# Banded attention with a context part: from a loop over head pairs to 16 unrolled steps of one block

## The chip, the cores and the metric

The kernel runs on one core of a Trainium2 chip. The metric is the device time of one launch in microseconds (us), the median of several runs. PE is the matrix engine (TensorE), DVE the vector engine, ACT the scalar engine, SP the engine whose queue issues the DMAs, PEld the loading of weights into PE.

## What is computed

The program is one inference step of a two-layer trunk with a width of 1024, for 512 latent and 128 context tokens (640 columns in all). Every layer has a gated feed-forward part, a mixer, and a second feed-forward part. The mixer of layer 0 has one input projection of 21 tiles of 128 columns: 4 tiles of attention queries (8 heads of 64, two heads a tile), 1 of keys, 1 of values (2 key/value heads), and 15 that belong to a recurrent mixer (RWKV-7). The attention part, cut to what matters:

```python
# queries in blocks of 128; keys: all context keys, a sink logit per head, and the
# latent keys of the block before, the same and the next one, masked to +-128 tokens
s_ctx = einsum("bqkgd,blkd->bkgql", qi, k_ctx) * scale
s_win = einsum("bqkgd,blkd->bkgql", qi, kw) * scale
parts = [where(valid, s_win, -inf), s_ctx, sink_s]
p = softmax(concatenate(parts, axis=-1), axis=-1)
out = einsum(p_win, vw) + einsum(p_ctx, v_ctx)      # latent queries and keys are rotated first
```

The 128 context tokens attend to context keys only and are not rotated. The recurrent mixer shifts its own 15 tiles by one token both ways (`_token_shift`). Both outputs go through one output projection.

## The kernel before, in words

Activations lie with channels on the 128 partitions and the 640 tokens along the free dimension. Every product with a weight matrix goes slab by slab (128 output columns): SP loads the slab, ACT and DVE split it in a high and a low part (`split_hi`, `split_lo`), PE makes 48 matmuls of 320 columns, and a consumer takes the result out of the accumulator banks (`pp[0]` to `pp[3]`, two banks each). Slabs lie in rings of four.

In the input projection of layer 0 (`AB_COLUMN` gives the order of its columns: queries, then the 15 recurrent tiles, then keys and values last), ACT takes a result to a padded buffer `praw` (L2167 to L2169), and DVE forms the token shift from it for all 21 tiles (L2410, L2414; for attention tiles the shift weights are 0). `ab_shift` counts these operations.

Attention is written by hand with semaphores; each engine works its own list in order. PE (`pe_attn_ab`) first waits for the last shifted tile, turns context keys and values (L377, L378, L380), copies keys to both halves of the partitions by matmuls with tables (L383 to L389), and then loops over 4 head pairs. In one turn of the loop it makes the rotated partner of the queries by a matmul (L397), the scores of one head of the pair for all four blocks and the context (L409 to L411), those of the other head, and per head 15 turnings of 128x128 in two parts (L420) and 15 products with the values (L435). DVE (`dve_attn_ab`) rotates the queries (L505 to L508), scales and masks the scores into SBUF (L514, L516), takes the maxima (L522), and divides the exponentials by their sums (L530 to L536). ACT takes exponentials (L467), copies turned maps (L475, L477, L478) and writes the result (L490, L491). Each stage handles a whole head, and the scores of the next turn of the loop wait for the end of the one before.

After attention comes the recurrent mixer. SP (`sp_rwkv`) loads its masks (L651) and its starting states (L653) once attention has ended; the first work of PE there (L857) waits for both.

The mixer of layer 1 (`pe_attn_c` and its partners, L1664 to L1956) is not changed. It already works in 32 unrolled steps of one block, with the turning three steps behind the scores, and rotates by DMA from partition to partition (L1652) with DVE operations inside its input projection. It comes into the prediction as the nearest thing to measure by.

Of the kernel before, what the change touches and what calls it, by code (L numbers as in the profile page):

```python
# [54 lines left out]
AB_COLUMN = [0, 1, 2, 3] + list(range(6, 21)) + [4, 5]  # L55
# [80 lines left out]
def build(nc, T):  # L136
    ctx = ExitStack()
    with ctx:
# [197 lines left out]
        a_keys = hh[:, 0:1280].rearrange("p (g n) -> p g n", g=2)  # L336
        a_pkeys = hh[:, 1280:1536].rearrange("p (g n) -> p g n", g=2)
        a_vtok = hh[:, 1536:2176].rearrange("p (t n) -> p t n", n=P)
        a_vpast, a_kpast = hh[:, 2176:2304], hh[:, 2304:2432]
        a_kpast_t, a_kout = hh[:, 2432:2560], hh[:, 2560:2688]  # L340
        a_sink = hh[:, 2688:2696]
        a_q, a_qp = hh[:, 2700:3212], hh[:, 3212:3340]
        a_t1, a_t2 = hh[:, 3340:3852], hh[:, 3852:4364]

        a_max, a_neg, a_es, a_den, a_rden = ([hh[:, o + 8 * i:o + 5 + 8 * i] for o in (4400, 4448)] for i in range(5))
        a_sk = hh[:, 4440:4442]
        a_s, a_e = ([o[:, q:q + 2560].rearrange("p (b n) -> p b n", b=5) for o in (hl, work)] for q in (0, 2560))
        a_pt = wh[:, 0:2048]
# [3 lines left out]
        PIECES = [(b, i) for b in range(NB) for i in range(ENDS[b] // P)] + [(NB, 0)]  # L352

        a_load, a_pe, a_act, a_dve, a_out = (sem(f"a_{n}") for n in ("load", "pe", "act", "dve", "out"))
        APE0 = Steps(a_pe, ["past_t", "v_t", "dup", "dup2"])
        AAC0 = Steps(a_act, ["past_t", "v_t", "dup2"])
        ADV0 = Steps(a_dve, ["mul0", "keys0", "mul1", "keys1"])
        APE = Steps(a_pe, ["rot", "sc0", "sc1", "ta0", "tb0", "pv0", "ta1", "tb1", "pv1"], 4)
        AAC = Steps(a_act, ["qp", "exp0", "pa0", "exp1", "pb0", "o0", "pa1", "pb1", "o1"], 3)
        ADV = Steps(a_dve, ["rope1", "rope", "s0", "mx0", "ng0", "s1", "dn0", "rd0", "pn0", "mx1", "ng1", "dn1", "rd1", "pn1"], 4)  # L360
        HALF_PIECES = 8
        IN_AB = start["in", 0, 0, 0]
        IN_C = start["in", 1, 0, 0]

        def sp_attn_ab(sp):
            sp.wait_ge(slab_used, IN_AB + AB_TILES + RING)
            sp.dma_start(a_vpast, T["cache_a_v"][0, 0].rearrange("t g d -> t (g d)")).then_inc(a_load, 16)
            sp.dma_start(a_kpast, T["cache_a_k"][0, 0].rearrange("t g d -> t (g d)")).then_inc(a_load, 16)
            sp.dma_start(a_sink, T["a_sink"].to_broadcast([P, AH])).then_inc(a_load, 16)
            sp.wait_ge(a_act, AAC0.value("v_t"))  # L370
            sp.dma_start(T["new_a_k"][0, 0].rearrange("t g d -> t (g d)"), a_kout).then_inc(a_out, 16)
            sp.dma_start(T["new_a_v"][0, 0].rearrange("t g d -> t (g d)"), a_vtok[:, 4, :]).then_inc(a_out, 16)

        def pe_attn_ab(pe):
            pe.wait_ge(a_load, 48)
            pe.wait_ge(ab_shift, 3 * AB_TILES)
            nc.tensor.transpose(pp[0][:, 0, 0:P], a_kpast, ident)  # L377
            nc.tensor.transpose(pp[0][:, 0, P:2 * P], big[:, T_KA, LAT:TOK], ident).then_inc(APE0.sem("past_t"), 1)  # L378
            for t in range(NCH):
                ins = nc.tensor.transpose(pp[1][:, t // 4, (t % 4) * P:(t % 4 + 1) * P], big[:, T_VA, t * P:(t + 1) * P], ident)  # L380
            ins.then_inc(APE0.sem("v_t"), 1)
            for g in range(2):
                nc.tensor.matmul(pp[2][:, g, :], dup[g], big[:, T_KA, 0:LAT], start=True, stop=True)  # L383
                ins = nc.tensor.matmul(pp[3][:, g, :], rdup[g], big[:, T_KA, 0:LAT], start=True, stop=True)
            ins.then_inc(APE0.sem("dup"), 1)
            pe.wait_ge(a_act, AAC0.value("past_t"))
            for g in range(2):
                nc.tensor.matmul(pp[0][:, g, 0:P], dup[g], a_kpast_t, start=True, stop=True)
                ins = nc.tensor.matmul(pp[0][:, g, P:2 * P], dup[g], big[:, T_KA, LAT:TOK], start=True, stop=True)  # L389
            ins.then_inc(APE0.sem("dup2"), 1)  # L390

            for g in range(2):
                with pe.Fori(0, 2) as jj:
                    it = jj + 2 * g
                    pe.wait_ge(a_act, AAC.before(it) - 1)
                    pe.wait_ge(a_dve, ADV.before(it))
                    nc.tensor.matmul(pp[2][:, 0, :], rot, big[:, it, 0:LAT], start=True, stop=True).then_inc(APE.sem("rot"), 1)  # L397
                    for h in range(2):
                        r = slice(h * HD, h * HD + HD)
                        if h == 0:  # L400
                            pe.wait_ge(a_dve, ADV.value("rope", it))
                            pe.wait_ge(a_act, AAC.value("qp", it))
                        else:
                            pe.wait_ge(a_dve, ADV.value("s0", it))
# [2219 lines left out]
```

## Time and profile before

| what | us |
| --- | --- |
| runs | 3267.14, 3279.99, 3290.77 |
| median | 3279.99 |
| the profiled execution, its own time | 3279.32 |
| its span, first to last instruction | 3277.5 |
| its PE busy / DVE busy / ACT busy | 3026.0 / 1618.2 / 934.7 |

The profile is of one execution. Times in it count from the start of its span. Matmuls of 32-bit floats appear as two records each (so "x30" in rows of L435 is 15 matmuls, and "x2" of L410 one); turnings appear as one. "PEclk" is the clock granted to PE as a share of 2.4 GHz: 1.00 and 0.50 are the two levels, and a value between them is a stretch with both.

### The profile page before, as it was taken

How to read it: one execution, taken by the hardware profiler on the slowest of the kernel's cores; microseconds unless marked ns; L12 is line 12 of the kernel's file. 1: busy time of each engine (PE TensorE's matmuls, PEld its weight loads, DVE VectorE, ACT ScalarE, POOL GpSimd, SP SyncE). 2: the span in 40 equal slices, each digit the busy share in tenths (PEclk: the TensorE clock that was granted, in tenths of full speed). 3: DMA queues.
4: the chain of work that ended last, by engine and by line, in shares of the span. 5: the costliest groups of instructions: out<-in, count | busy, mean ns of one | idle time of the engine just before them, and what ended most of it. 6: DMA issues, size and time to landing. Idle time of an engine off the chain costs nothing.

```text
span 3277.5 us, 65384 instructions
## 1 busy us (share of the span) xinstructions
PE 3026.0 (92%) x28476; PEld 2886.5 (88%) x28476; DVE 1618.2 (49%) x2444; ACT 934.7 (29%) x1597; POOL 0.2 (0%) x4
## 2 busy tenths in 40 slices
PE   7799999997669888899999999999999888999998
PEld 7799999995557776799999999999999668999998
DVE  2455465653445565455454656454633674422324
ACT  1221212322244342231222322212322573322222
POOL 0000000000000000000000000000000000000000
PEclk6799999997668899899999999999999899999999
DMA  6344454220000000234444344443342202222221
GB/s 207 91 111 127 115 142 116 71 58 4 0 19 5 5 6 5 84 97 133 124 123 116 103 116 122 116 135 110 105 112 71 59 1 65 74 74 71 77 77 58
DMA packets 394624, 270.71 MB, mean 83 GB/s; under 512 B 12315, under 2 KB 373046, under 8 KB 394294
## 3 DMA queue, kind: packets, MB, share of 16 engines
q1 hardware_dynamic: 394422, 267.74, 29.2%
q8 instruction: 161, 2.64, 0.3%
q14 instruction: 41, 0.34, 0.0%
HBM read 257.61 MB, written 4.06 MB: 80 GB/s over the span
## 4 chain that ended last, share of the span: by engine, by line
PE 87%; DVE 7%; ACT 3%; issue 2%; DMA 1%; SPq 0%; DVEq 0%; ACTq 0%
PE banks L2509 66%; PE banks L2533 2%; PE banks L1679 2%; PE banks L2464 2%; PE banks L843 1%; PE banks L435 1%; PE banks L410 1%; PE banks L826 1%; PE banks L1731 1%; DVE big L2309 1%; PE banks L837 1%; PE banks L2540 1%; PE banks L420 1%; DVE h_lo_as_f L1423 1%; PE banks L2519 1%
## 5 line engine op out<-in xcount | busy, mean ns | idle before, releaser
L2509 PE MATMUL banks<-h_hi,w_hi 128*128 128x320 f32 x3600 | 822.1, 310 | 11.5 <-DVE w_lo L2208 10.9
L2509 PE MATMUL banks<-h_lo,w_hi 128*128 128x320 f32 x3600 | 821.2, 309 | 0.0
L2509 PE MATMUL banks<-h_hi,w_lo 128*128 128x320 f32 x3600 | 820.4, 309 | 0.0
L2509 PEld LDWEIGHTS banks<-h_hi,w_hi 128*128 128x128 f32 x3600 | 602.0, 188 | 12.7 <-issue 11.7
L2509 PEld LDWEIGHTS banks<-h_lo,w_hi 128*128 128x128 f32 x3600 | 602.8, 188 | 0.0
L2509 PEld LDWEIGHTS banks<-h_hi,w_lo 128*128 128x128 f32 x3600 | 602.8, 188 | 0.0
L2509 PE MATMUL banks<-big_as_f32r,w_hi 128*128 128x320 f32 x2816 | 530.9, 310 | 5.8 <-DVE w_lo L2208 5.3
L2208 DVE TENSOR_TENSOR w_lo<-raw,w_hi 128x1024 fp32r<-128x1024 f32 x333 | 399.0, 1218 | 193.3 <-ACT w_hi L2088 192.6
L2088 ACT ACTIVATE w_hi<-raw 128x1024 fp32r<-128x1024 f32 x333 | 341.6, 1050 | 445.5 <-DMA raw<-ffn_w 290.4
L2509 PEld LDWEIGHTS banks<-big_as_f32r,w_hi 128*128 128x128 f32 x2816 | 443.7, 189 | 6.8 <-DVE w_lo L2208 6.1
L2353 DVE TENSOR_TENSOR work<-work,banks 128x640 f32<-128x640 f32 x88 | 72.2, 821 | 607.1 <-PE banks L2509 593.1
L2509 PE MATMUL banks<-big_as_f32r,w_lo 128*128 128x320 f32 x1408 | 321.9, 310 | 0.0
L2289 DVE SCALAR_TENSOR_TENSOR big<-work,cols,big 128x1024 f32<-128x1024 f32 x240 | 296.4, 1278 | 0.0
L2142 ACT ACTIVATE big_as_f32r<-work 128x640 f32 (+1 forms) x88 | 65.0, 739 | 616.4 <-DVE work L2353 616.4
L2509 PEld LDWEIGHTS banks<-big_as_f32r,w_lo 128*128 128x128 f32 x1408 | 236.4, 189 | 0.0
L2382 DVE SCALAR_TENSOR_TENSOR x<-banks,mod,x 128x320 f32<-128x320 f32 x336 | 127.0, 433 | 212.6 <-PE banks L2509 212.1
L2140 ACT ACTIVATE work<-banks 128x640 f32<-128x640 f32 x88 | 62.0, 704 | 281.3 <-PE banks L2509 250.6
L2356 DVE TENSOR_TENSOR big_as_f32r<-work,big_as_f32r 128x640 f32 (+1 forms) x88 | 72.7, 826 | 88.9 <-ACT big_as_f32r L2142 88.9
L2155 ACT ACTIVATE work<-x 128x640 f32<-128x640 f32 x48 | 35.5, 739 | 204.4 <-DVE x L2382 204.4
L2533 PE MATMUL banks<-h_hi,w_hi 128*128 128x320 f32 x192 | 52.0, 357 | 28.6 <-DVE w_lo L2208 17.5
L1679 PE MATMUL banks<-h_hi_as_f,big 64*128 64x512 f32 (+3 forms) x256 | 68.8, 527 | 8.6 <-issue 5.2
L2533 PEld LDWEIGHTS banks<-h_hi,w_hi 128*128 128x128 f32 x192 | 38.8, 228 | 30.2 <-DVE w_lo L2208 17.7
(354 smaller groups left out, 2744.6 us busy)
## 6 DMA issues: line engine op xcount, KB each, us to landing
raw<-ffn_w SPq DMA_DIRECT2D x272, 512.0 KB, 5.2
work<-mod_w SPq DMA_DIRECT2D x136, 512.0 KB, 3.8
raw<-w_in_c SPq DMA_DIRECT2D x24, 512.0 KB, 3.9
raw<-w_in_ab SPq DMA_DIRECT2D x21, 512.0 KB, 4.0
w_hi_as_f<-mod_w SPq DMA_DIRECT2D x8, 512.0 KB, 4.9
raw<-w_out_ab SPq DMA_DIRECT2D x8, 512.0 KB, 5.2
work<-big SPq DMA_DIRECT2D x64, 64.0 KB, 2.7
raw<-w_out_c SPq DMA_DIRECT2D x8, 512.0 KB, 5.3
```

The costliest lines, as they stand in the source:

```text
L1679: return mm(c_scores(b)[:, m, a:z], big[heads[m], h, b * P:(b + 1) * P], c_keys[h][heads[m], a:z], start=True, stop=True)
L2088: nc.scalar.activation(w_hi[:, j % RING, :, :], raw[:, j % RING, :, :], ACT.Copy).then_inc(hi_full, 1)
L2140: nc.scalar.activation(silu_t, pp[(n0 + 2 * e) % 4][:, :, 0:HALF], ACT.Silu).then_inc(silu_done, 1)
L2142: nc.scalar.activation(halves2(g_hi, 2 * i + e), prod_t, ACT.Copy).then_inc(ghi_done, 1)
L2208: nc.vector.tensor_tensor(w_lo[:, j % RING, :, :], raw[:, j % RING, :, :], f32(w_hi[:, j % RING, :, :]), ALU.subtract).then_inc(lo_full, 1)
L2289: nc.vector.scalar_tensor_tensor(out=sm, in0=sec_ring[:, e, :], scalar=cols3[:, k + (C_COND + DT * g), :], in1=sm, op0=ALU.mult, op1=ALU.a ...
L2353: nc.vector.tensor_tensor(prod_t, silu_t, pp[(n0 + 2 * e + 1) % 4][:, :, 0:HALF], ALU.mult).then_inc(pair_free, 2)
L2356: nc.vector.tensor_tensor(halves2(g_lo, 2 * i + e), prod_t, f32(halves2(g_hi, 2 * i + e)), ALU.subtract).then_inc(g_ready, 1)
L2382: ins = nc.vector.scalar_tensor_tensor(out=x[:, j, a:b2], in0=src, scalar=mod[:, gate + j, g:g + 1], in1=x[:, j, a:b2], op0=ALU.mult, op1= ...
L2464: ins = nc.tensor.matmul(pp[2 + j // 4][:, 0, 2 * (j % 4):2 * (j % 4) + 2], mod_ring[:, j % RING, k, :], cond[:, k, :], start=(k == 0), st ...
L2509: ins = nc.tensor.matmul(ps[:, c, 0:HALF], w, v[:, k, c * HALF:(c + 1) * HALF], start=(k == 0 and w is hi and v is xh), stop=(k == kts - 1 ...
L2533: nc.tensor.matmul(pp[j % 4][:, c, 0:HALF], w[:, j % RING, k, :], h_hi[:, k, c * HALF:(c + 1) * HALF], start=(k == 0 and w is w_hi), stop= ...
```

## The change

- The projection makes queries, keys and values first (`A_ORDER`, slabs 0 to 5); ACT copies these six straight into `big`, without token shift. The 15 recurrent tiles follow, with the shift as before.
- Queries and keys are rotated inside the projection: SP copies the partner rows of each tile with 8 DMAs (L395), DVE makes three operations of 512 columns for one tile (L540 to L544) at each of slabs 6 to 10. Keys are copied to both halves of the partitions by four DMAs (L401). The matmuls with tables go.
- Attention is 16 unrolled steps: one block of 128 queries for both heads of a pair. PE turns the map of step g-3, makes scores of step g, then multiplies values of step g-3. DVE adds the mask in the banks, takes a negated maximum of both heads in one operation, and scales the exponentials of step g-2. ACT copies out step g-4, the turned map of g-3, and takes exponentials of g-1 straight from the banks. The context queries of a pair ride on its fourth block.
- The masks and states of the recurrent mixer are loaded as soon as the last slab of the projection has been used; PE and DVE wait for the last result of attention by `A_END`.

```diff
-AB_COLUMN = [0, 1, 2, 3] + list(range(6, 21)) + [4, 5]
+        A_ORDER = [0, 1, 2, 3, T_KA, T_VA] + list(range(4, T_KA))
+        def sp_in_ab(sp, j):
...
+            i = j - 8
+            if 0 <= i < 5:
+                sp.wait_ge(pair_free, IN_AB + i + 1 + RING)
+                if i > 1:
+                    sp.wait_ge(ADR.s, ADR.value("q", i - 2))
+                for g in range(8):
+                    o = (g ^ 1) * 16
+                    sp.dma_start(a_rt[i % 2][g * 16:g * 16 + 16, :], big[o:o + 16, A_ORDER[i], 0:LAT]).then_inc(a_rot[i % 2], 16)
...
+            def scores(g):
+                it, b = a_at(g)
+                kv = it // 2
+                if g >= 2:
+                    it2, b2 = a_at(g - 2)
+                    pe.wait_ge(AAE.s, AAE.value(f"e{b2}", it2))
...
+                for h in range(2):
+                    r = heads[h]
+                    q, ps = big[r, it, b * P:(b + 1) * P], a_scores(g)[:, h, :]
+                    if joined:
+                        ins = mm(ps[:, 0:ENDS[b]], q, a_keys[r, kv, 0:ENDS[b]], start=True, stop=True)
+                    else:
+                        ins = mm(ps[:, P:ENDS[b]], q, a_keys[r, kv, P + k0 * P:P + k1 * P], start=True, stop=True)
...
+            def turn(g):
+                it, b = a_at(g)
+                pe.wait_ge(ADN.s, ADN.value(f"p{b}", it))
...
+                for h in range(2):
+                    for c in range(4 if b else 3):
+                        ins = tp(A_TURN[:, h, c * P:c * P + P], a_e[g % 2][:, h, c * P:c * P + P], ident)
...
+            def values(g):
...
+                for i, (c, t) in enumerate(ps):
+                    v = a_vpast[:, kv] if t is None else a_vtok[:, t, kv]
+                    for h in range(2):
+                        ins = mm(a_result(g)[heads[h], 0:P], v, a_pt[g % 2][:, h, c:c + P], start=(i == 0), stop=(i + 1 == len(ps)))
...
+            for g in range(ASTEPS + ALAG):
+                if g >= ALAG:
+                    turn(g - ALAG)
+                if g < ASTEPS:
+                    scores(g)
+                if g >= ALAG:
+                    values(g - ALAG)
...
+            def exps(g):
...
+                act.wait_ge(ADM.s, ADM.value(f"z{b}", it))
+                af(a_es[:, it, b:z, :], a_sn[:, it, b:z, :], ACT.Exp)
+                for bb in range(b, z):
+                    c0_, c1_ = (0, ENDS[b]) if bb == b else (384, 512)
+                    for h in range(2):
+                        ins = af(a_e[g % 2][:, h, c0_:c1_], a_scores(g)[:, h, c0_:c1_], ACT.Exp, bias=a_neg[:, it, bb, h:h + 1],
+                                 scale=SCALE, accum_out=a_den[:, it, bb, h:h + 1])
...
+            for g in range(ASTEPS + ALAG):
+                if g > ALAG:
+                    out(g - ALAG - 1)
+                if g >= ALAG:
+                    turned(g - ALAG)
+                if 1 <= g <= ASTEPS:
+                    exps(g - 1)
+            out(ASTEPS - 1)
...
+            i = j - 6
+            if 0 <= i < 5:
...
+                v.tensor_tensor(a_t1, big[:, t, 0:LAT], cos, ALU.mult).then_inc(ADR.sem("c"), 1)
+                dve.wait_ge(a_rot[i % 2], 128 * (i // 2) + 128)
+                v.tensor_tensor(a_rt[i % 2], a_rt[i % 2], sin, ALU.mult).then_inc(ADR.sem("s"), 1)
+                dve.wait_ge(ADR.s, ADR.value("s", i))
+                v.tensor_tensor(big[:, t, 0:LAT], a_t1, a_rt[i % 2], ALU.add).then_inc(ADR.sem("q"), 1)
...
+            def maxima(g):
...
+                dve.wait_ge(APS.s, APS.value(f"s{b}", it))
...
+                v.tensor_tensor(part, part, mask, ALU.add).then_inc(ADM.sem(f"k{b}"), 1)
...
+                ins = v.tensor_reduce(a_nmx[:, it, b, :], ps[:, :, 0:ENDS[b]], AX.X, ALU.max, negate=True)
...
+            for g in range(ASTEPS + 2):
+                if g >= 2:
+                    share(g - 2)
+                if g < ASTEPS:
+                    maxima(g)
...
         def sp_rwkv(sp):
             sp.wait_ge(lo_full, IN_AB + AB_TILES + RING)
-            sp.wait_ge(a_act, AAC.before(4))
+            sp.wait_ge(slab_used, IN_AB + AB_TILES + RING)
```

On DVE, inside one turn of the loop of the kernel before (one head pair; `h_lo_as_f_50` holds the first head's scores and `work` the second's), there stands:

```order
L514 SCALAR_TENSOR_TENSOR h_lo_as_f_50<-banks,attn 128x384
L514 SCALAR_TENSOR_TENSOR h_lo_as_f_50<-banks,attn 128x512 x2
L514 SCALAR_TENSOR_TENSOR h_lo_as_f_50<-banks,attn 128x384
L516 TENSOR_SCALAR h_lo_as_f_50<-banks 128x128
...
L522 TENSOR_REDUCE h_hi_as_f_49<-h_lo_as_f_50 128x1 x5
...
L525 TENSOR_SCALAR h_hi_as_f_49<-h_hi_as_f_49 128x5
```

On DVE at the same place of the changed kernel, for one step of a middle block (`banks` holds the scores of both heads, `h_hi_as_f_49` the exponentials):

```order
L561 TENSOR_TENSOR banks<-banks,attn 128x4x128
L563 TENSOR_REDUCE w_lo_as_f_53<-banks 128x2
L569 SCALAR_TENSOR_TENSOR w_lo_as_f_53<-w_lo_as_f_53,work 128x2
L572 TENSOR_TENSOR w_lo_as_f_53<-w_lo_as_f_53,work 128x2
L578 TENSOR_TENSOR w_lo_as_f_53<-w_lo_as_f_53 128x2
L580 RECIPROCAL w_lo_as_f_53<-w_lo_as_f_53 128x2
L586 TENSOR_SCALAR h_hi_as_f_49<-h_hi_as_f_49,w_lo_as_f_53 128x512 x2
```

A whole head's five pieces per operation have become one block of both heads: mask, one maximum, four small operations, two scalings.

On PE, the attention loop of the kernel before (`h_hi_as_f_49` rotated queries and keys, `h_lo_as_f_50` the map of a head), from the scores of the second head to the first head's values:

```order
L410 MATMUL banks<-h_hi_as_f_49 128x384
L409 MATMUL banks<-h_hi_as_f_49 128x128
L410 MATMUL banks<-h_hi_as_f_49 128x256
L411 MATMUL banks<-h_hi_as_f_49 128x128
...
L420 MATMUL banks<-base,h_lo_as_f_50 128x128 x8
...
L420 MATMUL banks<-base,h_lo_as_f_50 128x128 x7
L435 MATMUL banks<-w_hi_as_f_52,h_hi_as_f_49 64x128 x8
```

On PE in the changed kernel, two steps in a row (here `h_hi_as_f_49` is the map, `work` keys or values):

```order
L456 MATMUL banks<-base,h_hi_as_f_49 128x128 x8
L436 MATMUL banks<-work,big 128x384 x2
L470 MATMUL banks<-w_hi_as_f_52,work 64x128 x8
L456 MATMUL banks<-base,h_hi_as_f_49 128x128 x8
L436 MATMUL banks<-work,big 128x512 x2
L470 MATMUL banks<-w_hi_as_f_52,work 64x128 x8
```

Scores, turnings and products of different blocks now alternate, and "x2" is the two heads right behind each other.

On SP, around the end of the projection of the kernel before, and then of the changed one (`raw` takes weight slabs, and the recurrent mixer's masks after them):

```order
L1999 DMA raw<-w_in_ab 128x8x128 [waits lo_full] x21
L367 DMA h_hi_as_f_49<-cache_a_v 128x128 [waits slab_used]
L368 DMA h_hi_as_f_49<-cache_a_k 128x128
L369 DMA h_hi_as_f_49<-a_sink 128x8
L371 DMA new_a_k<-h_hi_as_f_49 128x128 [waits a_act]
L372 DMA new_a_v<-h_hi_as_f_49 128x128
L651 DMA raw<-t_rwkv 128x1600 [waits a_act,lo_full]
L653 DMA work<-state_b_wkv 64x8x64 x2
```

```order
L395 DMA work<-big 16x512 [waits ad_rope,pair_free]
L395 DMA work<-big 16x512 x7
L2040 DMA raw<-w_in_ab 128x8x128 [waits lo_full] x8
L401 DMA work<-big 64x640 [waits ad_rope]
L401 DMA work<-big 64x640 x3
L403 DMA new_a_v<-work 128x128 [waits aa_rows]
L404 DMA new_a_k<-work 128x128
L695 DMA raw<-t_rwkv 128x1600 [waits slab_used,lo_full]
L697 DMA work<-state_b_wkv 64x8x64 x2
```

The masks and states no longer wait for attention (`a_act`), and weight slabs stand behind rotation DMAs that wait for DVE (`ad_rope`).

## Rows read from the trace of the kernel before

**Rows 1.** Page, part 4: the chain that ended last, by engine

```profile
PE 87%; DVE 7%; ACT 3%; issue 2%; DMA 1%; SPq 0%; DVEq 0%; ACTq 0%
```

**Rows 2.** Busy time in 10 us stretches: PE, PEld, DVE, ACT, POOL, PEclk, DMA share, GB/s

```profile
815.00:825.00 10.00, 7.50 (x22) 5.47 (x21) 5.04 (x11) 1.07 (x4) 0.00 (x0) 0.50 0.00 0
825.00:835.00 10.00, 4.98 (x17) 3.49 (x15) 6.84 (x18) 2.62 (x9) 0.00 (x0) 0.50 0.00 0
```

**Rows 3.** The chain in order of time: start, length, what; the ends of attention

```profile
755.47 0.44 ACT work L2167
...
758.10 1.02 DVE big L2414 x2
...
926.71 0.27 ACT big L491
...
928.25 5.51 DMA work<-state_b_wkv
...
933.80 1.11 PE banks L857 x8
```

**Rows 4.** Durations of DVE and ACT, by line and form: busy, mean ns

```profile
L506 DVE TENSOR_TENSOR h_hi_as_f<-banks,attn 128x512 f32<-128x512 f32 x4 | 2.7, 682 | 0.0
L1889 DVE TENSOR_REDUCE w_lo_as_f<-banks 128x2 f32<-128x1280 f32 x32 | 47.7, 1491 | 32.8 <-PE banks L1679 23.1 <-PE banks L1682 9.7
L1891 DVE TENSOR_REDUCE w_lo_as_f<-banks 128x2 f32<-128x256 f32 x8 | 3.3, 414 | 0.0
L1900 DVE SCALAR_TENSOR_TENSOR w_lo_as_f<-w_lo_as_f,small 128x1 f32<-128x1 f32 x23 | 5.0, 219 | 0.8
L536 DVE TENSOR_SCALAR h_lo_as_f<-h_lo_as_f,h_hi_as_f 128x512 f32<-128x512 f32 x8 | 3.5, 478 | 0.0
L467 ACT ACTIVATE h_lo_as_f<-h_lo_as_f,h_hi_as_f 128x512 f32<-128x512 f32 x8 | 5.6, 706 | 0.0
L475 ACT ACTIVATE w_hi_as_f<-banks 128x1024 f32<-128x1024 f32 x8 | 8.2, 1024 | 30.3 <-PE banks L420 30.3
```

**Rows 5.** Pieces of PE on the chain: start, length, what

```profile
815.76 1.28 PE banks L410 x2
...
832.59 1.98 PE banks L420 x8
...
841.53 1.04 PE banks L420 x8
...
844.65 3.42 PE banks L435 x30
...
944.59 2.00 PE banks L725 x16
```

**Rows 6.** Layer 1's attention: timeline rows of PE and DVE

```profile
2640.53 1.35 PE L1679 MATMUL banks<-h_hi_as_f,big 64*128 64x512 f32 x6
...
2563.66 1.49 DVE L1889 TENSOR_REDUCE w_lo_as_f<-banks 128x2 f32<-128x1280 f32 x1 [2.00 <-PE banks L1682]
...
2579.98 1.49 DVE L1889 TENSOR_REDUCE w_lo_as_f<-banks 128x2 f32<-128x1280 f32 x1 [0.98 <-PE banks L1682]
```

**Rows 7.** Stretches of layer 1's attention and of the recurrent mixer

```profile
2551.00:2561.00 10.00, 8.81 (x32) 6.00 (x32) 5.90 (x11) 3.19 (x8) 0.00 (x0) 0.50 0.30 93
2571.00:2581.00 10.00, 9.88 (x66) 7.53 (x66) 7.35 (x13) 7.27 (x22) 0.00 (x0) 1.00 0.00 1
...
970.00:975.00 5.00, 3.04 (x126) 2.54 (x123) 2.31 (x7) 3.35 (x6) 0.00 (x0) 1.00 0.15 43
975.00:980.00 5.00, 3.71 (x87) 3.12 (x88) 3.60 (x7) 1.93 (x5) 0.00 (x0) 0.53 0.00 0
```

**Rows 8.** One slab of the input projection; SP in layer 1's projection

```profile
707.00:714.00 7.00, 7.00 (x50) 7.00 (x49) 3.85 (x7) 1.74 (x6) 0.00 (x0) 1.00 0.27 76
...
2443.89 5.05 SPq L1652 DMA_DIRECT2D work<-big  x8
```

More of the change, by code:

```diff
@@ L345, in build @@
[L345 to L348, printed above, removed]
+        heads = [slice(h * HD, h * HD + HD) for h in range(2)]
+        AGS = 2
+        ASTEPS = 4 * NB
+        ALAG = 3
+        A_ORDER = [0, 1, 2, 3, T_KA, T_VA] + list(range(4, T_KA))
+        A_OWN = 6
@@ new lines, in build @@
+        a_t1, a_rt = work[:, 0:512], [work[:, 512:1024], work[:, 5384:5896]]
+        a_keys = work[:, 1024:2560].rearrange("p (g n) -> p g n", g=2)
+        a_vtok = work[:, 2560:3200].rearrange("p (t n) -> p t n", n=P)
+        a_vpast, a_kpd, a_kout = work[:, 3200:3328], work[:, 3328:3584], work[:, 3584:3712]
+        a_sink, a_nsink = work[:, 5896:5904], work[:, 5904:5912]
+        a_e = [hh[:, 1024 * i:1024 * i + 1024].rearrange("p (h n) -> p h n", h=2) for i in range(2)]
+        a_pt = [wh[:, 1024 * i:1024 * i + 1024].rearrange("p (h n) -> p h n", h=2) for i in range(2)]
@@ L350, in build @@
+        a_nmx, a_neg, a_sn, a_es, a_den, a_rd = (
+            wl[:, 40 * i:40 * i + 40].rearrange("p (t b h) -> p t b h", t=4, b=NB + 1) for i in range(6))
+        band_sides = band[:, 0:512].rearrange("p (a two n) -> p a two n", two=2, n=P)[:, :, 1, :]
+        band_prev, band_next = band[:, P:2 * P], band[:, 3 * P:4 * P]
         WIN = [(max(0, b - 1), min(NB, b + 2)) for b in range(NB)]
         ENDS = [P + (k1 - k0) * P for k0, k1 in WIN]
-        PIECES = [(b, i) for b in range(NB) for i in range(ENDS[b] // P)] + [(NB, 0)]
@@ L361, in build @@
-        HALF_PIECES = 8
+        a_load, a_dup, a_lamb, a_out = (sem(f"a_{n}") for n in ("load", "dup", "sign", "out"))
+        a_rot = [sem(f"a_rot{i}") for i in range(2)]
+        per_b = lambda s: [f"{n}{b}" for b in range(NB) for n in s]
+        ADR = Steps(sem("ad_rope"), ["c", "s", "q"])
+        APK = Steps(sem("ap_rows"), ["k", "v", "o"])
+        AAK = Steps(sem("aa_rows"), ["k", "v", "o"])
+        APS, APT, APV = (Steps(sem(f"ap_{n}"), per_b(n[0])) for n in ("scores", "turns", "values"))
@@ L382, in pe_attn_ab @@
[L382 to L389, printed above, removed]
@@ new lines, in pe_attn_ab @@
+            mm, tp = nc.tensor.matmul, nc.tensor.transpose
+            pe.wait_ge(a_load, 64)
+            pe.wait_ge(pair_free, IN_AB + AB_TILES + RING)
+            for g in range(AGS):
+                ins = tp(A_TURN[:, 0, g * P:g * P + P], a_kpd[:, g * P:g * P + P], ident)
+            ins.then_inc(APK.sem("k"), 1)
+            for t in range(NCH):
+                ins = tp(pp[3][:, t // 4, t % 4 * P:t % 4 * P + P], big[:, T_VA, t * P:(t + 1) * P], ident)
+            ins.then_inc(APK.sem("v"), 1)
@@ L590, in build @@
         w_hsel = blk[:, 0:P:HD]
-        heads = [slice(h * HD, h * HD + HD) for h in range(2)]
         quads = [(h, p) for h in range(2) for p in range(2)]
```

326 lines of the change are left out of this document (143 added, 183 removed).

## The prediction

> **What bounds the kernel now.** I read the chain that ended last first: PE holds 87% of it [rows 1], nearly all weight slabs that the change leaves alone. So the question is what the attention of layer 0 costs between two slabs, and the chain in order of time gives its ends [rows 3]. The projection's last slab is done at 755.45 (ACT takes it at 755.47), DVE ends its token shift at 759.12 (758.10+1.02), attention writes its last result at 926.98 (926.71+0.27). SP then loads masks and states; the last transfer lasts 5.51 and ends at 933.76, and PE starts the recurrent mixer at 933.80. From 755.45 to 933.80 are 178.3 us. The stretches inside say what kind of time it is [rows 2]: in the scores' part PE is busy 7.5 of 10 us at clock 0.50 with DVE at 5.0, in the next 5.0 with DVE at 6.8 and ACT at 2.6. No engine is full. They wait for each other, head by head, and the gaps keep PE at its lower level. The limit is the serial order, which the change rewrites.
>
> **Prices of one new step.** I take a middle block; the first block has 384 keys instead of 512, the last adds the context queries.
>
> DVE. The mask is added over 512 elements: an operation with one operand in the banks takes 0.68 [rows 4], 0.72 with its gap. Writing back to the banks is not in this trace; the bound below is 0.5 (a bit under the row), above twice the row, 1.4; I take the row. The maximum runs over 1024 elements. From 1280 elements in 1.49 and 256 in 0.41 [rows 4] one element costs 1.05 ns, so 1.22, with gap 1.26. Four small ones at up to 0.22 each [rows 4] make 0.83. Two scalings of 512 at 0.48 [rows 4], with a little overlap 0.84. Sum 3.65. The first block comes to 3.0 (256 masked, 768 compared, two of 384), the last to 3.7; four blocks 14.0, sixteen 56.0, or 3.5 a step.
>
> ACT. Two exponentials of 512 at 0.71, a turned map of 1024 at 1.02, a result at 0.27 [rows 3, 4], a small exponential and gaps 0.3: 3.0 a step.
>
> PE. A turning costs 0.25 at the lower level and 0.13 at the upper (8 in 1.98 and in 1.04) [rows 5]. The scores of one head of 384 keys take 1.28 at the lower level [rows 5], 3.33 ns a key. Whether two heads, which lie on different halves of the rows, run beside each other, layer 1 shows: three pieces, 512 keys of one map and 256 and 384 of the other, take 1.35 at the upper level [rows 6]. In series their 1152 keys would need 1.92 at half of 3.33 ns, the longer map alone 1.07. They overlap for the most part, so a pair of 512 costs 1.71 low and 0.85 high. The values: before, 15 products on the same half of the columns take 3.42 at the upper level, 0.23 each; 8 products that alternate between the halves take 2.00 at the lower level in the recurrent mixer [rows 5], 0.50 a pair where a series would take 0.9. The new code alternates, so I take 0.5 low and 0.25 high a pair. With 7.5 turnings, 470 keys and 3.75 pairs as means: 5.3 at the lower level, 2.7 at the upper. So at the upper level DVE sets the pace (3.5), at the lower PE does (5.3).
>
> **The path, start to end.** The token shift of the last tile still runs to 759.12 on DVE, since a recurrent tile is last now; PE's preparation (8 turnings instead of turnings and the matmuls with tables) fits beside it. DVE's first maximum starts at 759.15. From there DVE has 56.0 of work, of which the shares of the last two steps (2.8) come after its last maximum: 812.35. Then the tail in series: exponentials of the last step 2.3, share 1.55, turning 1.05, copy 1.05, values 1.0, result 0.4, which gives 819.7. That is the floor. Added: PE has its first scores done by 759 and its first map to turn at 764.6 (below), an idle stretch of some 5 us in which it goes to the lower level, and it is then the bound for two steps, 3. One more low stretch on the way, 3. Friction of the in-order lists 0.1 a step, 2: layer 1 needs 4.08 a step ((2579.98-2563.66)/4) [rows 6] with PE busy 9.88 of 10 [rows 7]. A tail at the lower level, 1.3. Attention then ends at 829.
>
> **The loads.** Masks and states are issued at 755.5 instead of 927. Their landing, 6.8 from 926.98 to 933.80 [rows 3], lies under 70 us of attention, so PE starts the recurrent mixer at 829.1. What is late next is ACT, whose tanh and sigmoid of two tiles ran under that landing; they are now beside PE's first 3 us of work and I cost them at nothing, at most 1.
>
> **The projection.** A slab takes PE 7.04, and PE is full, 7.00 of 7.00, with DVE busy 3.85 and ACT 1.74 [rows 8]. At five slabs DVE gets three more operations of 512 columns, 3 x 0.68 [rows 4], 2.0: 5.9 of 7.04, still under PE. Each rotation holds SP for 5.05 (8 DMAs) [rows 8], and slabs 11 to 13 are queued on SP behind one that waits for DVE's rotation two tiles earlier. That puts a slab's load at most one slab late, with two in hand. Layer 1 runs the same pattern. Cost 0, bound above 35 (five slabs at 7.04 each).
>
> **Sum.** 933.8-829.1 = 104.7 saved of the profiled execution's 3279.3: 3174.6, so 3175. The median of the runs stands 0.7 above that execution, and the runs spread by 0.4% either way; so about 1% is what a measurement of this kernel can tell from no change.
>
> **The rivals.**
> 1. PE stays low throughout. For it: attention before sat at 0.50 with PE busy 7.5 of 10 [rows 2], and in the recurrent mixer a stretch with 3.04 of 5 busy was followed by 0.53 [rows 7]. DVE's pace at the upper level would leave PE busy only 2.7 of 3.5, 77%. Against it: at the lower level PE has no gaps at all, and layer 1 went from 0.50 at 8.81 of 10 busy to 1.00 [rows 7]. Price: PE from 764.6 (the first map is ready for turning: 759.15 plus two maxima, 1.9 and 2.4, and a share, 1.1) 16 x 5.3 less 3 steps' scores (4.8), 844.6; with tail and friction 849, time 3195.
> The Trainium skill (TensorE: Matmul & The Clock Gate, Part 4: PE-mode transpose) says that turnings in transpose mode do not engage the full clock because they do not count as busy in the same way. By that rule the third of the new PE work that is turning would not help to keep the upper level, and this rival's 3195 would be the time. The chance above goes by rows: at 841.53 eight turnings do run at the upper level, 0.13 each, behind products [rows 5].
> 2. DVE is dearer than the nearest rows say: the mask, written back to the banks, at 1.4 instead of 0.72. No row speaks for or against. Price: 16 x 0.7 = 11, time 3186. Column halves that don't overlap for values cost PE 0.9 a step at the upper level, 3.6 against DVE's 3.5; about the same price.
> 3. Slabs late in the projection, by the waits that SP now has in its list. For it: SP's order. Against it: 1.1 us of slack on DVE and two slabs in hand. Price up to 35: 3210.
> 4. The steps don't overlap, and the kernel gets slower. Its place is the ring PE, DVE, ACT, DVE, PE, ACT, PE, ACT of one step: scores 1.7, maximum 2.4, exponentials 1.7, share 1.25, turning 2.0, copy 1.05, values 2.0, result 0.3 at the lower level, 12.4. For it: in-order lists with single buffers for the turned map. Against it: two banks of scores, and exponentials are awaited two steps back. Price: 16 x 12.4 = 198 from 757.4, end 956, 22 later than now: 3301. It makes the kernel slower once a step exceeds (933.8-757.4)/16 = 11.0.
> The Trainium skill (TensorEngine Tiling (Array Packing), Key Properties) also says that a change of tiling mode drains PE. Each step now has three modes. No row isolates a drain; by the rule PE's price would rise somewhat, and the forecast, in which DVE sets the pace, would stand as long as a drain stays under 0.25.
>
> **Chances.** The forecast with its additions more or less, 3165 to 3184: 0.64. Rival 1: 0.15. Rival 2: 0.13. Rival 3: 0.05. Rival 4: 0.03, of which half a result within 1% (3301 is 0.6% above 3280) and half beyond. Faster by over 1% (under 3247): 0.97; within 1%: 0.02; slower by over 1%: 0.01. The range starts at 3150 (a floor of 3165 less half a per cent of spread) and reaches 3205 (rival 1 with a little spread).
>
> **What would show it.** Right: maxima of successive steps start 3.4 to 3.8 apart in stretches at clock 1.00, DVE has hardly a gap there, and 5 to 6 apart at 0.50 with PE full; the mask row reads about 0.7, the maximum 1.22, pairs of scores 0.85; PE starts the recurrent mixer near 829 with no DMA wait; PE stays 7.00 of 7.00 through the projection. Wrong: PEclk at 0.50 over most of attention, a mask far above 0.7, DVE waiting for ACT at each step, or PE gaps at slabs 10 to 14 released by a DMA of `w_in_ab`.

## The result, and the profile after

The changed kernel takes 3163.08 us (median of 4 runs, 3152.56 to 3168.47) against 3279.01 for the kernel before (4 runs, 3267.14 to 3290.77): a ratio of 0.9639, 95% interval 0.9609 to 0.9669. The forecast was 3175 with a range of 3150 to 3205. The time was inside the range, and 12 us under the forecast. Of the runs further down one is left out of its median: `values_late` has five runs from 3149.81 to 3169.98 and a slow one of 3691.81, with PE's granted clock at 0.73 over the whole.

The page of the changed kernel, first its span and busy times, then its chain by engine:

```profile
span 3162.5 us, 65085 instructions
...
PE 2965.2 (94%) x28421; PEld 2838.0 (90%) x28421; DVE 1594.0 (50%) x2398; ACT 928.4 (29%) x1579; POOL 0.2 (0%) x4
...
PE 87%; DVE 7%; ACT 3%; issue 2%; DMA 1%; SPq 0%; ACTq 0%; DVEq 0%
```

The chain by engine has the same shares as [rows 1], although 115.0 us have gone from the span (3277.5 to 3162.5). Shares over the whole span can't show what one stage does, so the stage has to be read by itself. Its chain in order of time (start, length, what), at the start of attention, over one middle step, and to its end:

```profile
754.78 0.44 ACT work L2212
...
758.42 0.35 DVE banks L561
758.80 0.97 DVE w_lo_as_f L563
...
766.95 0.44 DVE banks L561
...
786.68 0.62 DVE banks L561
787.32 1.24 DVE w_lo_as_f L563
788.58 0.17 DVE w_lo_as_f L569
788.78 0.16 DVE w_lo_as_f L572
788.94 0.08 DVE w_lo_as_f L578
789.04 0.18 DVE w_lo_as_f L580
789.24 0.75 DVE h_hi_as_f L586 x2
789.99 0.62 DVE banks L561
790.63 1.24 DVE w_lo_as_f L563
...
805.75 0.89 DVE h_hi_as_f L586 x2
...
806.69 1.11 PE banks L456 x8
807.82 1.03 ACT w_hi_as_f L509
808.90 1.09 PE banks L470 x16
809.99 1.05 PE banks L456 x8
811.07 1.03 ACT w_hi_as_f L509
812.15 1.09 PE banks L470 x16
813.24 1.04 PE banks L456 x8
...
816.52 0.39 ACT big L515
817.05 0.68 PE banks L901 x8
```

Two things are to be seen. From 766.95 to 806.64 every piece of the chain is DVE's, here the step from one maximum to the next of 3.31 (787.32 to 790.63; its two scalings belong to the block before, a first block with 384 keys). And the tail is not one last step: from 806.69 on, turning, copy and products follow each other three times on PE and ACT, some 3.2 us each, while DVE finishes the last maximum and two shares beside them, off the chain. Beside [rows 3]: the end of the projection moved from 755.47 to 754.78, and the first work of the recurrent mixer from 933.80 to 817.05. The stage shrank from 178.3 to 62.3 us, and these 116 us are the whole gain.

They divide so. Preparation (end of projection to first scores on PE) took 17.7 us before (755.47 to 773.21) and takes 2.0 now (754.78 to 756.75): 15.7, read from the two profiles alone, since no run takes the preparation apart. The landing of masks and states at the end, 6.8, is gone but for 0.1: 6.7. The loop itself, from there to the end of the last result, went from 153.8 (773.21 to 926.98) to 60.2 (756.75 to 816.91): 93.6.

Stretches of 10 us of the changed kernel (busy time of PE, PEld, DVE, ACT, POOL, then PEclk, DMA share, GB/s):

```profile
755.00:765.00 10.00, 5.39 (x32) 3.39 (x32) 8.98 (x20) 6.01 (x17) 0.00 (x0) 0.91 0.52 134
765.00:775.00 10.00, 9.68 (x89) 7.05 (x88) 9.44 (x28) 8.12 (x25) 0.00 (x0) 0.92 0.01 2
775.00:785.00 10.00, 9.48 (x94) 6.89 (x94) 9.45 (x27) 8.67 (x26) 0.00 (x0) 1.00 0.00 0
785.00:795.00 10.00, 9.21 (x94) 6.59 (x90) 9.52 (x27) 7.90 (x22) 0.00 (x0) 1.00 0.01 2
...
805.00:815.00 10.00, 6.35 (x72) 4.92 (x69) 6.06 (x22) 6.81 (x20) 0.00 (x0) 1.00 0.00 0
```

Against [rows 2], where PE was busy 7.5 and 5.0 at clock 0.50 and DVE 5.0 and 6.8, three engines now work at once: PE at 9.2 to 9.7, DVE at 9.5, ACT at 7.9 to 8.7, at clock 1.00 up to the end of attention, except for a short stretch before 767.

Durations of the new pieces between 755 and 825, by form (busy in all, mean ns), which answer to [rows 4]:

```profile
L563 DVE TENSOR_REDUCE w_lo_as_f<-banks 128x2 f32<-128x1024 f32 x8 | 9.8, 1224 | 0.3
...
L561 DVE TENSOR_TENSOR banks<-banks,attn 128x512 f32<-128x512 f32 x8 | 5.5, 693 | 0.0
```

The mask written back to the banks costs what the nearest row said (0.69 against 0.68), and the maximum of 1024 the interpolated 1.22.

### The profile page after: what moved, and what is told of

Same layout as the page of the kernel before. It is cut to its first block, busy times and chain, and to the rows that moved or that the text cites. A ratio compares the mean times of both kernels' runs of the same rounds, so it can differ in the third digit from the quotient of the medians.

```text
span 3162.5 us, 65085 instructions
## 1 busy us (share of the span) xinstructions
PE 2965.2 (94%) x28421; PEld 2838.0 (90%) x28421; DVE 1594.0 (50%) x2398; ACT 928.4 (29%) x1579; POOL 0.2 (0%) x4
## 4 chain that ended last, share of the span: by engine, by line
PE 87%; DVE 7%; ACT 3%; issue 2%; DMA 1%; SPq 0%; ACTq 0%; DVEq 0%
PE banks L2556 68%; PE banks L2580 2%; PE banks L2511 2%; PE banks L1722 2%; PE banks L887 1%; PE banks L2587 1%; PE banks L1774 1%; PE banks L881 1%; PE banks L870 1%; DVE h_lo_as_f L1467 1%; DVE big L2354 1%; PE banks L769 1%; DMA raw<-ffn_w 1%; PE banks L2566 1%; PE banks L956 1%
## 5 line engine op out<-in xcount | busy, mean ns | idle before, releaser
L2556 PE MATMUL banks<-h_hi,w_hi 128*128 128x320 f32 x3600 | 821.9, 309 | 11.4 <-DVE w_lo L2253 10.9
L2580 PEld LDWEIGHTS banks<-h_hi,w_hi 128*128 128x128 f32 x192 | 40.1, 235 | 30.2 <-DVE w_lo L2253 17.7
```

The lines of the kernel that those rows point to most:

```text
L2556: ins = nc.tensor.matmul(ps[:, c, 0:HALF], w, v[:, k, c * HALF:(c + 1) * HALF], start=(k == 0 and w is hi and v is xh), stop=(k == kts - 1 ...
L2580: nc.tensor.matmul(pp[j % 4][:, c, 0:HALF], w[:, j % RING, k, :], h_hi[:, k, c * HALF:(c + 1) * HALF], start=(k == 0 and w is w_hi), stop= ...
```

## The experiments

The time of whole runs of one kernel scatters by some 10 us either way, and much of that lies outside the stage: in the profiled executions span less stage is 3084.5 us in sink_act, 3100.2 in the changed kernel and 3110.4 in lag2. So beside each ratio to the kernel before I read the stage from the profile: its length (ACT taking the last slab, to PE's first work of the recurrent mixer), the mean distance between the starts of successive maxima (15 distances), and the tail from the start of the last maximum. The stage is known to 0.1.

| run | median us | ratio to before, 95% | stage | step | tail |
| --- | --- | --- | --- | --- | --- |
| changed kernel | 3163.08 | 0.9639, 0.9609-0.9669 | 62.3 | 3.21 | 10.0 |
| lag0 | 3299.54 | 1.0059, 1.0035-1.0083 | 193.2 | 11.87 | 11.0 |
| lag2 (2 runs) | 3222.72 | 0.9835, 0.9797-0.9874 | 116.6 | 6.49 | 15.1 |
| loads_wait | 3158.97 | 0.9643, 0.9605-0.9681 | 70.8 | 3.28 | 17.6 |
| values_series | 3162.18 | 0.9648, 0.9615-0.9680 | 67.5 | 3.44 | 11.9 |
| dve_more | 3173.95 | 0.9687, 0.9657-0.9718 | 72.4 | 3.81 | 10.8 |
| pe_more | 3167.93 | 0.9680, 0.9655-0.9705 | 67.1 | 3.42 | 11.8 |
| act_more | 3155.11 | 0.9649, 0.9602-0.9697 | 63.5 | 3.28 | 10.3 |
| sink_act | 3150.32 | 0.9618, 0.9591-0.9644 | 60.3 | 3.07 | 10.1 |
| values_late | 3162.97 | 0.9650, 0.9625-0.9676 | 61.7 | 3.23 | 9.3 |
| late_sink | 3153.61 | 0.9627, 0.9601-0.9652 | 59.2 | 3.03 | 9.7 |

**Is it the overlap? lag0: the same instructions, one step after the other.**

```diff
-            for g in range(ASTEPS + ALAG):
-                if g >= ALAG:
-                    turn(g - ALAG)
-                if g < ASTEPS:
-                    scores(g)
-                if g >= ALAG:
-                    values(g - ALAG)
+            for g in range(ASTEPS):
+                scores(g)
+                turn(g)
+                values(g)
```

ACT's list becomes exps(g), turned(g), out(g), and DVE's maxima(g), share(g).

> The changed kernel with no overlap of steps by order: each engine does its part of step g before anything of step g+1. All instructions, their forms and the work in the projection are the same. Theory (the gain is overlap): one step is the ring scores 1.7, maximum 2.2, exponentials 1.6, share 1.15, turning 2.0, copy 1.03, values 2.0 with PE at its lower level and 0.3 of gaps, 12.0, in the mean of the four kinds of block 11.4; attention lasts some 185 instead of 62.3 us, so about 3163 + 120 = 3283, the time of the kernel before. Rival (the gain is the form: both heads in one operation, no copy of the scores, rotation out of the loop): a step stays under 5 and the time under 3163 + 30 = 3193.

The step is 11.87 us, the stage 193.2 (11.4 and 185 were expected), the whole a little slower than the kernel before, by 0.35 to 0.83%. The new instructions without the interleaving are worth nothing; the interleaving takes 8.7 us off each of 15 steps, 130 in all. This is rival 4 of the prediction, made to happen: its ring was priced at 12.4 a step and 3301 us, against 11.87 and 3299.54. The sum of the ring was sound at the lower level; the clock there was 0.50 to 0.67 in every 10 us. So the 130 us are overlap and the clock that comes with it, together.

**How far ahead must PE be? lag2.**

```diff
-        ALAG = 3
+        ALAG = 2
```

> The changed kernel, turning two steps behind the scores instead of three. Theory: turning of step g-2 then waits for the share of the same turn of the loop, and ACT's exponentials of g-1 stand behind the copy of it, which makes a ring share 1.15, turning 1.05, copy 1.03, exponentials 1.6 and gaps 0.2, about 4.9 a step instead of 3.3, with PE idle enough to fall to its lower level at times: 3163 + 26 = 3189 or somewhat more. Rival: DVE alone sets the pace, at 3.3 whatever the lag, and the time stays within 3 of 3163.

6.49 a step where about 4.9 was expected, and half the gain is gone. The ring is another one than expected, too. Its chain in order of time shows one full step:

```profile
783.34 1.96 PE banks L456 x8
785.30 1.84 PE banks L436 x4
...
787.17 0.71 DVE banks L561
...
787.90 1.24 DVE w_lo_as_f L563
...
789.83 0.76 DVE h_hi_as_f L586 x2
...
790.63 1.54 PE banks L456 x6
```

DVE does the maxima of step g before the share of step g-1. With a lag of two, PE's turning waits for that share, the next scores stand behind the turning, and the next mask waits for the scores: turning 1.96, scores 1.84, mask 0.71, maximum 1.24, small ones 0.6, scalings 0.76, with their gaps 7.3 (783.34 to 790.63), all in series. The clock of the half-idle PE moves between its levels (0.69 over 775 to 805; in the step shown 0.50 from 784 to 786 and 1.00 from 787 to 789), so that its part, 3.8 of those 7.3, takes nearly twice its time. A third step in flight takes the turning out of the ring, and that is worth 54 us of stage. Lag and clock count together: no run shows lag 2 at the upper level; with PE's part at 2.1 (turning 1.03, scores 1.06, from rows at 1.00) the step shown would be 5.6, an estimate, still far above 3.31.

**Who sets the pace? One more operation of 512 on DVE, on ACT, and four more turnings on PE, each in every step.**

```diff
 # dve_more, in maxima(g)
+                v.tensor_tensor(hl[:, g % 8 * 512:g % 8 * 512 + 512], cos, cos, ALU.mult)
                 v.tensor_tensor(part, part, mask, ALU.add).then_inc(ADM.sem(f"k{b}"), 1)
 # act_more, after the exponentials of exps(g)
+                af(hl[:, g % 8 * 512:g % 8 * 512 + 512], cos, ACT.Copy)
 # pe_more, in turn(g)
+                for c in range(4 if b else 3):
+                    tp(A_TURN[:, 0, c * P:c * P + P], a_e[g % 2][:, 0, c * P:c * P + P], ident)
```

> The changed kernel with one more DVE operation of 512 columns in each step, ahead of the mask (its result is not used). Theory: DVE sets the pace at 3.3 a step, so it shows in full: 16 x 0.62 = 10, 3173. Rival: PE's ring of turning, copy and values at 3.23 is the pace and DVE has hidden slack: well under 10, as PE rows in that case keep 3.3 apart.

> The changed kernel with four (in first blocks three) more turnings of 128x128 in each step, ahead of the others and into the same banks: 0.52 more in turning. Theory of a tie (PE's ring turning 1.05, ACT's copy 1.03, values 1.09 and gaps makes 3.23, beside DVE's 3.3): a step goes to 3.75, 16 x 0.45 = 7 more, 3170. Rival (DVE alone, and PE's own sum of 2.96 as the next): 2.96 + 0.52 = 3.48, 3 more, 3166.

> The changed kernel with one more ACT copy of 512 columns (0.58) in each step, behind the exponentials and after they are reported. Theory: ACT has about 0.4 of slack a step (2.9 of 3.3 by its starts), but the copy of the turned map, a part of PE's ring, comes behind it: 0.2 to 0.4 a step, 3 to 6 more, 3166 to 3169. Rival: the slack of ACT takes it all: no change, within 2 of 3163.

DVE's operation is paid in full: each distance of the steady part grows by 0.60, the stage by 10.2. ACT's costs nothing in the steady part, where 0.2 to 0.4 a step was expected: the later distances are 3.45, 3.31, 3.18, 3.25 with and without it. PE's four turnings (0.49 us) are paid in two kinds of block and not in the two others: the distances become 3.91, 3.68, 3.18, 3.25, and the stage is 4.8 longer, between the 3 and the 7 of the two expectations. So DVE is the bound, but in blocks of 512 keys PE stands right behind it. PE's list in pe_more shows why (timeline: start, length, what; PEld is the weight load of the products, with its wait):

```profile
785.55 0.66 PE L455 MATMUL banks<-base,h_hi_as_f 128*128 128x128 f32 x4
786.04 1.04 PE L458 MATMUL banks<-base,h_hi_as_f 128*128 128x128 f32 x8
787.01 1.13 PE L436 MATMUL banks<-work,big 64*128 64x512 f32 x4
788.19 0.85 PEld L472 LDWEIGHTS banks<-w_hi_as_f,work 128*64 128x64 f32 x16 [0.89 <-ACT w_hi_as_f L511]
788.20 1.09 PE L472 MATMUL banks<-w_hi_as_f,work 128*64 128x128 f32 x16
789.22 0.66 PE L455 MATMUL banks<-base,h_hi_as_f 128*128 128x128 f32 x4
```

Read from start to start: added turnings 0.49, turning 0.97, scores to values 1.19, values 1.02, 3.67 in all. In the changed kernel the same step takes 3.24 at the upper level (783.54 to 786.78), against DVE's 3.31. PE's rows touch, but the 1.19 is not the scores' own price: the products wait for ACT's copy of the turned map, which ends at 788.15. Where they don't have to wait for it, in values_late, the same pair of scores takes 1.06 (timeline):

```profile
782.31 1.13 PE L436 MATMUL banks<-work,big 64*128 64x512 f32 x4
783.37 1.09 PE L473 MATMUL banks<-w_hi_as_f,work 128*64 128x128 f32 x16
```

So what stands behind DVE is PE's ring with ACT's copy inside it (turning, copy, products), and PE's own work is some 0.1 less.

**Do the halves of the columns overlap? values_series: all products of one head, then those of the other.**

```diff
-                for i, (c, t) in enumerate(ps):
-                    v = a_vpast[:, kv] if t is None else a_vtok[:, t, kv]
-                    for h in range(2):
+                for h in range(2):
+                    for i, (c, t) in enumerate(ps):
+                        v = a_vpast[:, kv] if t is None else a_vtok[:, t, kv]
```

> The changed kernel with the products with the values in series by head (all pieces of one head, then of the other), not alternating. Theory: alternating lets the two halves of the columns run beside each other: eight records pairs take 1.09 now; in series they take 0.23 each, 1.8, as in the kernel before. PE's ring turning, copy, values (3.23 now, beside DVE's 3.3) grows to about 3.95, so 16 x 0.67 = 11 more, 3174. Rival 1: PE has slack beside DVE's 3.3 apart from its own sum (2.96 + 0.75 = 3.7): 7 more, 3170. Rival 2: halves don't overlap in either order: no change, values stay at 1.09.

They do. The row of a block's 8 products in this run, and the same row in the changed kernel (timeline):

```profile
786.53 1.58 PE L470 MATMUL banks<-w_hi_as_f,work 128*64 128x128 f32 x16
```

```profile
785.75 1.09 PE L470 MATMUL banks<-w_hi_as_f,work 128*64 128x128 f32 x16
```

From start to start the products take 1.52 in series (786.53 to 788.05 on PE) and 1.02 alternating, where 1.8 was expected in series: alternating saves 0.5 us of PE a block. It comes through where PE is level with DVE (distances 3.74, 3.73, 3.18, 3.24) and in the tail, some 4 us of stage; another 1 is a start at the lower clock. The stage as a whole is 5.2 longer, half of the 11 expected. The medians of whole runs (3162.18 and 3163.08) don't resolve it.

**What is the early load worth? loads_wait.**

```diff
         def sp_rwkv(sp):
...
-            sp.wait_ge(slab_used, IN_AB + AB_TILES + RING)
+            sp.wait_ge(*A_END)
             sp.dma_start(rw[:, 0:RWKV_W]
```

> The changed kernel, but the masks and starting states of the recurrent mixer are again loaded only when attention has ended (as in the kernel before). Theory: the hoisted loads are worth their whole landing, since nothing else was under it: before, 6.8 us lay between the last result of attention and the first work of the mixer, after 0.1. So 3163 + 7 = 3170, with a DMA row of 5.5 us alone on the chain. Rival: part of it is lost anyway, because ACT's tanh and sigmoid run under the landing: then 3163 + 4 or less.

Its chain at the end of attention (start, length, what):

```profile
817.34 0.39 ACT big L515
...
818.18 0.68 SPq L697
...
818.90 4.93 DMA work<-state_b_wkv
...
823.87 1.11 PE banks L901 x8
```

The landing is back on the chain: 6.1 us from the end of the result (817.73) to PE's start (823.87), against 0.1 (816.91 to 817.05) in the changed kernel. The stage is 8.5 longer; the other 2.5 are a slower start and a tail partly at the lower level (0.83 from 805 to 815). In the medians of whole runs nothing of it can be seen (3158.97 and 3163.08, where 3170 was expected), so that this part pays is shown in the stage of one profile alone.

**Does turning raise the clock? clock: between attention and recurrent mixer PE idles, makes 200 turnings, idles, and makes 100 products of 128 columns (200 records), while DVE multiplies in between.**

```diff
+            pe.wait_ge(x_idle, 1)
+            for _ in range(200):
+                ins = tp(bank(7)[:, 0:P], mean_d, ident)
+            ins.then_inc(x_done, 1)
+            pe.wait_ge(x_idle, 2)
+            for _ in range(100):
+                ins = mm(bank(7)[:, 0:P], mean_d, ident, start=True, stop=True)
```

> The changed kernel with two stretches put between attention and the recurrent mixer: DVE works some 14 us while PE waits, PE does 200 turnings of 128x128 back to back and nothing else, DVE works 14 us again, PE does 100 plain 32-bit float products of 128x128x128. Theory (the rows: PE held its upper level through attention though a third of its work is turning): turnings count as work, so they begin at 0.25 each (lower level) and go on at 0.13 each; 200 take about 30 us. Rival (the Trainium skill, TensorE: Matmul & The Clock Gate, Part 4: turnings don't count as busy in the same way): all 200 stay at 0.25, 50 us, and only the products go from 0.43 to 0.22.

The run takes 3227.67 us, one execution, with both stretches in it. The 200 turnings take 23.7 us, less than the 30 expected.

Stretches of 1 us, first around the rise in the turnings, then in the products (PE, PEld, DVE, ACT, POOL, PEclk):

```profile
833.00:834.00 1.00, 1.00 (x7) 1.00 (x6) 0.00 (x0) 0.00 (x0) 0.00 (x0) 0.50 0.00 0
834.00:835.00 1.00, 1.00 (x7) 1.00 (x6) 0.00 (x0) 0.00 (x0) 0.00 (x0) 0.59 0.00 0
835.00:836.00 1.00, 1.00 (x11) 1.00 (x10) 0.00 (x0) 0.00 (x0) 0.00 (x0) 1.00 0.00 0
...
875.00:876.00 1.00, 1.00 (x8) 1.00 (x7) 0.00 (x0) 0.00 (x0) 0.00 (x0) 0.61 0.00 0
876.00:877.00 1.00, 1.00 (x12) 1.00 (x11) 0.00 (x0) 0.00 (x0) 0.00 (x0) 1.00 0.00 0
```

After an idle stretch at 0.50, turnings and nothing else bring the granted clock to 1.00 and hold it (1.00 from 840 to 850, with nothing but turnings), and the count of a microsecond goes with it, from 7 to 11. Products do the same. The Trainium skill (TensorE: Matmul & The Clock Gate, Part 4: PE-mode transpose) says that the full clock doesn't engage for turnings in transpose mode; here it does, and the measurement decides. That these turnings are of that kind is not printed in the rows; what they show is one record for a turning where a 32-bit product leaves two.

**Can the bound be lowered? sink_act, values_late, late_sink.** sink_act takes the small addition of the sink off DVE and gives it to ACT as the bias of the exponential; DVE has one operation less a step, ACT one more. values_late makes the products of step g-4 where those of g-3 were, so that PE does not wait for ACT's copy of the turned map. late_sink does both. Of values_late only the order is shown; its waits move with it.

```diff
 # sink_act, on DVE
-                dve.wait_ge(ADM.s, ADM.value(f"n{b}", it))
-                v.tensor_tensor(a_sn[:, it, b:z, :], a_neg[:, it, b:z, :], sk, ALU.add).then_inc(ADM.sem(f"z{b}"), 1)
 # sink_act, on ACT
-                af(a_es[:, it, b:z, :], a_sn[:, it, b:z, :], ACT.Exp)
+                for h in range(2):
+                    af(a_es[:, it, b:z, h], a_neg[:, it, b:z, h], ACT.Exp, bias=a_sink[:, 2 * it + h:2 * it + h + 1])
 # values_late, on PE (ACT's copy-out moves one step later too)
-                if g >= ALAG:
-                    values(g - ALAG)
+                if g > ALAG:
+                    values(g - ALAG - 1)
```

> The changed kernel without DVE's addition of the sink to the negated maximum (L572, 0.2 a step with its gap); ACT takes exp(neg + sink) with two small exponentials instead of one. Theory of a tie: DVE goes from 3.3 to 3.1, but PE's ring keeps 3.23: at most 0.05 a step, 1 less, 3162. Rival (DVE alone sets the pace): 16 x 0.2 = 3 less, 3160.

> The changed kernel with PE's products with the values moved one step later (turn g-3, scores g, values g-4), so that they no longer wait for the copy of the map just turned. Theory of a tie: the ring goes, but DVE keeps its 3.3: no change in the middle; at the tail, where DVE is done and PE's ring alone took 3.25 a step, turnings come earlier by up to 1 each: 1 to 2 less, 3161 to 3162. Rival: nothing, or 1 more for the step that is added.

> Both: values one step later, and the sink's addition on ACT. Theory of a tie: now that both bounds move, DVE's 3.1 is the pace: 16 x 0.2 = 3 less and the tail's 1 to 2: 3158 to 3159, more than the two alone add up to. Rival (DVE alone): the sum of the two.

values_late alone leaves the step at 3.23: PE's wait for the copy (5.1 us from 770 to 806 in the changed kernel's waits, PEld at L470) had cost nothing, which agrees with DVE as the bound. sink_act brings the step from 3.21 to 3.07, so the ring of turning, copy and products, which takes 3.25 in the tail, doesn't cap the mean step, as the theory of a tie had it; the blocks of 384 keys have a shorter one. Both together give 3.03, 0.18 less than the changed kernel, which is the removed operation (0.16) and its gap. The 0.04 between them lies in the start: later the distances are 3.12, 2.98, 3.05, 3.27 with sink_act and 3.12, 2.99, 3.05, 3.25 with both, so that values_late adds nothing there. The stage is 60.3 with sink_act and 59.2 with both, against 62.3. Against the kernel before, sink_act has the lowest ratio measured, 0.9618; but its interval overlaps the changed kernel's, its profiled execution is 15.7 faster outside the stage and 2.0 inside, and that it beats the changed kernel rests on the stage in one profile of each, not on the runs.

## Why the prediction was right, point by point

- **The bound** was placed right: the serial order, not an engine. lag0 shows it from the other side.
- **First maximum**: 759.15 forecast, 758.80 measured. Two things nearly cancel here: the projection and with it the token shift end 0.70 earlier, and a mask of 0.38 with its gap, which the forecast did not put ahead of the first maximum, comes in.
- **DVE's step**: 3.65 for a middle block forecast. Measured: 3.31 from 787.32 to 790.63, with the scalings of a first block in it, and 3.43 as the sum of a middle block's own pieces. Mask to maximum 0.73 (0.72) and maximum 1.26 (1.26) were exact; four small ones came to 0.66 (0.83), since each took about 0.16 and not up to 0.22, and two scalings of 512 start 0.79 before the next mask (0.84; two of 384 start 0.67 before it). Four blocks are 13.2 instead of 14.0. The last maximum ended at 808.30 with its context part, not at 812.35 (before the additions): 4.05 of the 12.05 us by which the stage ended before the forecast.
- **A low stretch at the start, +3, and another on the way, +3.** The first came as foretold, if sooner and shorter: PE waited 3.04 us to 761.56, for ACT to free the banks of the third step's scores, and not some 5 for its first map; from 763 to 767 its clock then reads 0.59, 0.50, 0.50 and 0.70 by the microsecond. It cost 0.1 (the distances after the first are 3.32, 3.31, 3.24, 3.46, against 3.31, 3.18, 3.26, 3.45 later): PE's slow scores were in the banks when DVE had just finished the work before them. The second never came. This is the failed step: 6 us were added for slow stretches of PE as if PE were the bound through all of each, and 0.1 was paid. That it was so little is in part luck. loads_wait starts attention by the same instructions, but its low stretch is longer:

```profile
760.00:768.00 8.00, 5.62 (x41) 4.38 (x42) 7.58 (x19) 5.35 (x17) 0.00 (x0) 0.79 0.50 140
...
760.00:768.00 8.00, 7.46 (x46) 5.76 (x46) 7.31 (x23) 4.06 (x12) 0.00 (x0) 0.57 0.00 0
```

  The first line is the changed kernel's, the second that of loads_wait. There the same four distances are 3.31, 3.48, 3.63, 3.84, which is 1.1 more than later on, and in the run clock 1.2 more. There PE's slow products and turning (1.48 at 765.39, 1.32 at 766.87), and ACT's copy and exponentials behind them, stand on the chain ahead of DVE's work. In values_late, where the products are out of that ring, a low stretch as long (760 to 767) cost 0.3. So what a slow stretch of PE costs hangs on its length and on how little PE's ring has to spare beside DVE.
- **Friction, +2**: nothing. DVE is busy 9.5 of 10, and the distances repeat to 0.01.
- **PE's step**: 2.7 at the upper level was a mean. For a middle block its terms give 2.9, and 3.24 were measured (783.54 to 786.78). The scores of a pair of 512 take 1.06 of their own, not 0.85 (full overlap) nor 1.71 (none): the two row halves overlap by about three quarters. The row that the prediction took this from already said so: 1.35 where the longer side alone would need 1.07, which scaled to 512 keys is 1.07 (an estimate). The rest is a wait that the forecast left out: the products stand behind ACT's copy of the map just turned, with only the scores between them. This put PE level with DVE where the forecast had it a quarter idle. In the steady part it did not cost; in a longer low stretch it did, as above.
- **The tail**: 7.4 plus 1.3 at the lower level, 8.7; measured 8.75 (808.30 to 817.05), all of it at the upper level. Right by cancellation. The forecast follows only the last step's chain; in truth three steps were still to be turned when DVE's work on the 14th was done (806.64), and each cost 3.25 on PE and ACT in turn (turning, copy, products), since no other step's scores were left to cover the copy. Steps in flight are paid again at the end.
- **Sum of it**: 829.1 less 4.05 less the 8 of the three additions is 817.05, where the mixer starts.
- **The loads**: hidden, 0.1 where 6.1 stand in loads_wait (6.8 before). They are issued at 758.58 and 759.00, not at 755.5: on SP's queue they stand behind the copies of the new keys and values (L403, L404), which wait for ACT. With nearly 60 us to spare that costs nothing.
- **The projection**: cost 0, as forecast. Both kernels have PE full through the slabs with the rotation (50.0 of 50.0 from 650 to 700), and the last slab ends 0.7 earlier. That rules out rival 3.
- **Rival 1** (low clock throughout, 3195): fell, 1.00 from 767 to the tail. In lag2, where PE waits in the ring, the low clock is there for much of the time. In dve_more PE was busy 23.8 of 30 (775 to 805) at 1.00, in the kernel before 7.5 of 10 at 0.50 [rows 2]: the busy share at one level doesn't tell which level a rewritten stage will have. The drain at a change of tiling mode stays under the limit that the prediction set (0.25): by the rows of pe_more each piece of PE begins before the modelled end of the one before it, or 0.06 after where it waits for the copy.
- **Rival 2** (a mask of 1.4; columns in series): 0.69 and 1.09 for four pairs, so neither.

## What to carry to other kernels

Where engines wait for each other, price the new order as each engine's own list per step plus the first step's filling and the last steps' emptying, and charge a slow stretch of an engine that isn't the bound only with what is left once its lead is used up (here 0.1 to 1.2 us, where 6 was added). Then count the ring: with one step too few in flight (lag2) the same instructions cost twice as much a step, and the idle engine's lower clock comes on top. To find the bound of a stage with three busy engines, add the same small operation to each in turn and look at the distances in the trace, not at the medians, which scatter by more than such an effect.

## What was not expected of the hardware

- A run of turnings alone brings PE from 0.50 to 1.00, and holds it there (clock, above).
- Two score products of 512 columns on opposite halves of the rows take 1.06 for the pair at the upper level (values_late), where a full overlap would be 0.85 and none 1.71; eight value products on alternating halves of the columns take 1.02 from start to start, in series 1.52.
- One DVE addition that reads and writes the banks costs the same as one that reads them and writes SBUF: 0.69 and 0.68 for 512 columns.
